# Starting each bank of sums with its own first product instead of a product of zeros, in a two-block transformer kernel on one Trainium2 core

## The chip, the cores and the metric

The kernel runs as one program on one core of a Trainium2 chip. The time is that of the device for one execution, in microseconds (us). Engines are named as in the profile: PE is TensorE's matmul side and PEld its weight load, DVE is VectorE, ACT is ScalarE, POOL is GpSimd, SP is SyncE. A stage is a run of weight units, as listed below.

## The reference

Two blocks of two layers each work on a sequence of 256 tokens with 1024 channels, batch 1, in float32. Cut to its products, the computation is:

```python
# first block
h = h + short_conv_mixer(rmsnorm(h), sc_w_in, sc_w_conv, sc_w_out)     # layer 0
h = h + squared_relu_mlp(rmsnorm(h), mlp_w_up[0], mlp_w_down[0])       # 1024 -> 4096 -> 1024
h = h + sigmoid(rmsnorm(h) @ ple_w_gate[0]) * (p[0] @ ple_w_proj[0])
h = h + dilated_attention_mixer(rmsnorm(h), positions, attn_w_qkv, attn_w_o)   # layer 1
h = h + squared_relu_mlp(...)
h = h + sigmoid(...) * (...)
x = rmsnorm(h, norm_final)
# second block
h = h + 0.5 * swiglu(rmsnorm(h), ffn1_w_in[0], ffn1_w_out[0])          # 1024 -> 2 x 2816 -> 1024
h = h + s5_mixer(rmsnorm(h), ...)                                      # state space, then a gated product
h = h + 0.5 * swiglu(rmsnorm(h), ffn2_w_in[0], ffn2_w_out[0])
kv = shared_kv(h, ...)
h = h + 0.5 * swiglu(rmsnorm(h), ffn1_w_in[1], ffn1_w_out[1])
h = h + nsa_mixer(rmsnorm(h), kv, w_qg, q_norm, w_o, rel_bias)         # sparse attention, 16 heads
h = h + 0.5 * swiglu(rmsnorm(h), ffn2_w_in[1], ffn2_w_out[1])
```

## The kernel before

**Units.** All large weight matrices are cut into 280 units of 128 x 2048 float32 numbers (1 MB each), used in a fixed order. The stages and their numbers of units are sc_in 12, sc_out 4, mlp0 32, ple0 5, qkv 36, wo 4, mlp1 32, ple1 5, ffn0 33, glu 4, ffn1 33, kv 6, ffn2 33, qg 4, nwo 4, ffn3 33. A unit comes through a ring of three slots: SP loads it (`raw`), ACT rounds it to float32r (`w_hi`, L1173), DVE subtracts to get the rest (`w_lo`, L1974), and PE uses both. ACT's step waits until PE is through with the unit three back (`unit_done`), PE waits for DVE's (`lo_ready`).

**Split products.** The activations are split the same way (`x_hi`, `x_lo`, ACT L1173 and DVE L1981). One product of a 128 x 128 block of weights and 256 tokens is made of three matmuls, in `exact` (L476 to L482): high by high (L480), high by low (L481), low by high (L482). A unit is 16 such triples, 48 matmuls of 256 columns.

**Banks of sums.** PSUM has eight banks of 128 x 512 float32, here called DB[0] to DB[3], U[0], U[1], MB and XB. A bank holds two blocks of 256 columns side by side (two blocks of output channels by 256 tokens). There are four ways in which units fill banks:
- `up_unit` without `arrive` (L529 to L535): first block over all eight chunks of the contraction, then the second block. Each block's first triple has start=True. No product of zeros.
- `up_unit` with `arrive` (L514 to L528), the first unit of a stage (13 calls: sc_out, mlp0, ple0, qkv, mlp1, ple1, ffn0, glu, ffn1, kv, ffn2, qg, ffn3): chunks outside, blocks inside, because the chunks of x arrive one pair after the other; before each pair PE waits for a semaphore (L518). Both blocks are open at once. The bank is begun by a product of zeros over its whole width, with start=True (L515), and every real product has start=False. It stands behind the wait for the unit's weights (`lo_ready`, L512) and ahead of the first wait for a chunk. `first_unit` (L496) does the same for the first of all.
- `down_unit` (L551): each unit adds two chunks of the contraction to all eight blocks of output, in DB[0] to DB[3], over 16 units (mlp) or 11 (ffn). Ahead of the first down unit of each mlp and ffn stage, `clear_sums` (L567) begins the four banks by four products of zeros. In `mlp` it stands behind the wait for `rs_ready` and ahead of the waits for `relu_ready` (L639 to L641), in `ffn` behind several waits (L688 to L695) and ahead of the down unit's own waits for weights and hidden values (L553, L554).
- The output projections of both attentions: `out_unit` (L877) adds to the four banks `WO` and begins each with a product of zeros (L888), in the first unit, behind a wait per bank. `out_part` (L1121) adds one chunk at a time to DB[2] and DB[3], begun at step 5 of the heads' loop (L1147); the third unit has DB[0], begun at L1159.

The product of zeros reads `zero`, a bfloat16 tile: 128 x 128 by 128 x 512. `clear_sums` has one more call, ahead of the S5 stage's sums (L917), and `keep_warm` (L572) makes such products at the start and around the S5 stage (26 + 20 + 6 + 24); `fin_sums` has a narrow one (L729).

**Order.** PE's order is written out by hand and has no planner. Between units stand the small products of norms (`norm_sum` L582, `norm_bcast` L588: sums over channels, then the spread of the result, with POOL and DVE between), the S5 tables' transposes (`table_turn`, L608, in mlp0 and mlp1), the attention's scores, transposes and values, and for the sparse attention a loop over 16 heads (L1139 to L1154) of `n_scores` (L1074 to L1079), `n_values` (L1106 to L1113), `n_turn` (L1093, L1094) and `out_part`. A stage ends with DVE adding the sums to h (L1987), ACT and DVE splitting the new x chunk by chunk, and the next stage's first unit taking each pair of chunks as it comes.

The split product and the clear in the code:

```python
nc.tensor.matmul(out, a_hi, b_hi, start=start, stop=False, skip_group_check=True)   # L480
nc.tensor.matmul(out, a_hi, b_lo, start=False, stop=False, skip_group_check=True)   # L481
return nc.tensor.matmul(out, a_lo, b_hi, start=False, stop=stop, skip_group_check=True)   # L482
...
for b in range(4):                                                                  # L569
    nc.tensor.matmul(DB[b], zero[:, 0:P], zero[:], start=True, stop=False, skip_group_check=True)
```

## Time and profile before

| | |
|---|---|
| median of 3 runs | 1874.66 us (1873.47 to 1879.29) |
| the profiled execution | 1871.93 us, of which the span is 1869.8 us |
| granted PE clock, mean over the span | 0.991 |
| PE busy | 1819.2 us (97%) in 15362 matmuls |
| DVE, ACT, POOL busy | 1202.9, 865.7, 627.8 us |
| DMA queues | 336.58 MB moved |

The span is cut from one profiled execution; the runs of the median were made without a profile. "Idle before" in a row is the time for which the engine did nothing before the instruction, with the instruction that ended it. Matmul rows overlap: a matmul of 256 columns has a duration of 0.28 us but the next one starts 0.11 to 0.12 us later, so costs are read from start to start. The matmul records of some products are missing from the trace, their weight loads (PEld) are there.

### The profile page before, as it was taken

The numbers are of one execution on the slowest core, as the hardware profiler recorded it, in microseconds if no ns is written. First come the engines' busy times: TensorE is split into PE (matmuls) and PEld (weight loads), VectorE is DVE, ScalarE is ACT, GpSimd is POOL, SyncE is SP. The second block draws the span as 40 slices with busy tenths as digits, with TensorE's granted clock in tenths as the row PEclk, the third lists the DMA queues.
The fourth block names the chain that finished last, engine by engine and source line by source line (L and its number), as shares of the span: only waits on it lengthen the run. The fifth ranks groups of instructions, "written<-read, shape, count | busy, mean of one in ns | idle before, by whom it ended". The sixth has DMA issues, their size and how long they took to land.

```text
span 1869.8 us, 35519 instructions
## 1 busy us (share of the span) xinstructions
PE 1819.2 (97%) x15362; PEld 1771.9 (95%) x15386; DVE 1202.9 (64%) x1380; ACT 865.7 (46%) x1096; POOL 627.8 (34%) x756
## 2 busy tenths in 40 slices
PE   8899999999999999999999889999999999999999
PEld 7899999999999999999999779999899999789999
DVE  7877667666664666686655855556655657756554
ACT  5254445544444544464344254344554446764442
POOL 6977781486752887010000620000000003530000
PEclk9999999999999999999999999999999999899999
DMA  7456665454444556557555416656346653024552
GB/s 262 171 203 217 220 230 190 156 180 170 159 167 155 182 208 219 200 207 305 181 183 211 148 47 217 216 211 216 137 136 209 216 199 124 23 69 181 184 194 97
DMA packets 53799, 336.58 MB, mean 180 GB/s; under 512 B 7899, under 2 KB 11020, under 8 KB 16908
## 3 DMA queue, kind: packets, MB, share of 16 engines
q1 hardware_dynamic: 46272, 300.00, 45.1%
q10 hardware_dynamic: 3276, 19.64, 2.9%
q0 software_dynamic: 4096, 14.68, 2.3%
q8 instruction: 121, 1.98, 0.4%
q14 instruction: 34, 0.28, 0.0%
HBM read 318.54 MB, written 15.75 MB: 179 GB/s over the span
## 4 chain that ended last, share of the span: by engine, by line
PE 83%; DVE 9%; ACT 4%; POOL 2%; issue 2%; DMA 1%; SPq 0%; ACTq 0%; DVEq 0%; POOLq 0%
PE psum L480 25%; PE psum L481 24%; PE psum L482 24%; DVE w_lo L1974 3%; ACT w_hi L1173 2%; DVE both L1981 1%; POOL swap L1891 1%; PE psum L1076 1%; PE psum L980 1%; ACT both L1173 1%; PE psum L942 1%; DVE yc L2312 1%; DVE h L1987 1%; PE psum L1093 1%; PE psum L1074 1%
## 5 line engine op out<-in xcount | busy, mean ns | idle before, releaser
L480 PE MATMUL psum<-both,w_hi 128*128 128x256 f32 x3584 | 1015.6, 283 | 21.7 <-DVE both L1981 12.8
L482 PE MATMUL psum<-both,w_lo 128*128 128x256 f32 x3584 | 1003.1, 280 | 0.0
L481 PE MATMUL psum<-both,w_hi 128*128 128x256 f32 x3584 | 1003.1, 280 | 0.0
L1974 DVE TENSOR_TENSOR w_lo<-raw,w_hi 128x2048 fp32r<-128x2048 f32 x277 | 655.7, 2368 | 287.7 <-ACT w_hi L1173 286.7
L1173 ACT ACTIVATE w_hi<-raw 128x2048 fp32r<-128x2048 f32 (+1 forms) x281 | 535.3, 1907 | 579.1 <-PE psum L482 561.1
L480 PEld LDWEIGHTS psum<-both,w_hi 128*128 128x128 f32 x3584 | 683.4, 191 | 26.6 <-DVE both L1981 15.7
L481 PEld LDWEIGHTS psum<-both,w_hi 128*128 128x128 f32 x3584 | 676.2, 189 | 0.9 <-issue 0.2
L482 PEld LDWEIGHTS psum<-both,w_lo 128*128 128x128 f32 x3584 | 675.4, 188 | 0.0
L1723 POOL TENSOR_TENSOR ssum<-sq 128x512 f32<-128x512 f32 x11 | 17.6, 1596 | 729.3 <-ACT sq L1197 729.3
L480 PE MATMUL psum<-hid_hi,w_hi 128*128 128x256 f32 x640 | 180.7, 282 | 0.0
L481 PE MATMUL psum<-hid_lo,w_hi 128*128 128x256 f32 x640 | 179.2, 280 | 0.0
L482 PE MATMUL psum<-hid_hi,w_lo 128*128 128x256 f32 x640 | 179.2, 280 | 0.0
L480 PEld LDWEIGHTS psum<-hid_hi,w_hi 128*128 128x128 f32 x640 | 122.3, 191 | 1.3 <-issue 0.8
L481 PEld LDWEIGHTS psum<-hid_lo,w_hi 128*128 128x128 f32 x640 | 120.2, 188 | 0.1
L482 PEld LDWEIGHTS psum<-hid_hi,w_lo 128*128 128x128 f32 x640 | 120.1, 188 | 0.0
L2111 DVE TENSOR_TENSOR tc<-psum,rs 128x512 f32<-128x512 f32 x44 | 30.4, 692 | 58.5 <-PE psum L482 58.5
L2105 DVE TENSOR_TENSOR ta<-psum,rs 128x512 f32<-128x512 f32 x44 | 30.4, 691 | 57.2 <-PE psum L482 56.3
L480 PE MATMUL psum<-w_hi,both 128*128 128x256 f32 x224 | 63.7, 284 | 1.4 <-DVE src L2525 1.4
L1895 POOL TENSOR_TENSOR qk<-qk,swap 32x512 f32<-32x512 f32 x24 | 63.6, 2651 | 1.9
L1891 POOL TENSOR_TENSOR swap<-swap,sin_rs 32x512 f32<-32x512 f32 x24 | 44.4, 1848 | 58.9 <-DVE swap L2384 58.9
L482 PE MATMUL psum<-w_hi,both 128*128 128x256 f32 x224 | 62.6, 279 | 0.0
L481 PE MATMUL psum<-w_lo,both 128*128 128x256 f32 x224 | 62.5, 279 | 0.0
(397 smaller groups left out, 2078.2 us busy)
## 6 DMA issues: line engine op xcount, KB each, us to landing
raw<-in_weights SPq DMA_DIRECT2D x279, 1024.0 KB, 4.8
table<-tables ACTq DMA_DIRECT2D x8, 1792.0 KB, 9.6
tables<-st POOLq DMA_DIRECT2D x16, 512.0 KB, 4.2
tables<-st POOLq DMA_DIRECT2D x8, 256.0 KB, 4.8
tables<-turns POOLq DMA_DIRECT2D x8, 256.0 KB, 4.4
w<-in_cmp_w ACTq DMA_DIRECT2D x4, 512.0 KB, 5.5
tbl<-in_cmp_w ACTq DMA_DIRECT2D x4, 512.0 KB, 5.6
tbl<-bias_v SPq DMA_DIRECT2D x128, 16.0 KB, 4.8
```

Source lines behind the costliest of these rows:

```text
L480: nc.tensor.matmul(out, a_hi, b_hi, start=start, stop=False, skip_group_check=True)
L481: nc.tensor.matmul(out, a_hi, b_lo, start=False, stop=False, skip_group_check=True)
L482: return nc.tensor.matmul(out, a_lo, b_hi, start=False, stop=stop, skip_group_check=True)
L942: last = nc.tensor.matmul(y_of(c, jj), x5[c % 2][:, ri, jj, 0:SK], q_[:, jj, ri], start=False, stop=ri == 1, skip_group_check=True)
L980: last = nc.tensor.matmul(DB[half][0:2 * NCMP, 0:P], blk[rows, l, :, :].rearrange("p c n -> p (c n)"), [w1, w1v][kind][rows, l, :], start= ...
L1074: nc.tensor.matmul(bank[:, 0:P], q[:, 0:P], ks[rows, br, a, 0:P], start=True, stop=True, skip_group_check=True)
L1173: copy = lambda out, in_, **kw: nc.scalar.activation(out, in_, ACT.Copy, **kw)
L1891: pool.tensor_tensor(swap[:], swap[:], sin_rs[0:32].unsqueeze(1).broadcast_to([32, 2, SEQ]), ALU.mult).then_inc(sem["sin_part"], 1)
L1895: pool.tensor_tensor(qk[0:32, side, gr], qk[0:32, side, gr], swap[:], ALU.add).then_inc(sem["qk_ready"], 1)
L1974: tt(w_lo[:, g % RING], raw[:, g % RING], w_hi[:, g % RING].bitcast(F32), ALU.subtract).then_inc(sem["lo_ready"], 1)
L2105: tt(ta[:], two(A_BANK), rs_b, ALU.mult).then_inc(sem["a_scaled"], 1)
L2111: tt(tc[:], two(B_BANK), rs_b, ALU.mult).then_inc(sem["b_gated"], 1)
```

## The change

A bank is begun by the first real product that goes into it: this product gets start=True, and the product of zeros in front is left out. Where two blocks of a bank are open together, only the first block's first triple starts; the second block's first triple keeps start=False. This is done in `first_unit`, in `up_unit` with `arrive`, in the down units of mlp and ffn (`down_unit` gets a flag `first`), in `out_unit`, in `out_part` and in the third unit of the last projection. The waits stay where they are. `clear_sums` stays for the S5 stage, as do `keep_warm` and `fin_sums`.

```diff
--- before.py
+++ after.py
@@ -496,7 +496,6 @@
             def first_unit(bank):
 
                 ws = slot(0)
-                nc.tensor.matmul(bank, zero[:, 0:P], zero[:], start=True, stop=False, skip_group_check=True)
                 for c in range(KC):
                     if c == KC // 2:
                         pe.wait_ge(sem["lo_ready"], 1)
@@ -504,7 +503,7 @@
                         pe.wait_ge(sem["xl_ready"], XBASE[R_IN] + c // 2 + 1)
                     for m in range(2):
                         last = exact(bank[:, m * SEQ:(m + 1) * SEQ], wide(ws, c, m),
-                                     (x_hi[0][:, c], x_lo[0][:, c]), False, c == KC - 1)
+                                     (x_hi[0][:, c], x_lo[0][:, c]), c == 0 and m == 0, c == KC - 1)
                 last.then_inc(sem["unit_done"], 1)
 
             def up_unit(g0, k, x, bank, arrive=None, mid=None, with_chunk=None):
@@ -512,13 +511,12 @@
                 pe.wait_ge(sem["lo_ready"], g0 + 1 + RING * k)
                 ws = slot(g0)
                 if arrive is not None:
-                    nc.tensor.matmul(bank, zero[:, 0:P], zero[:], start=True, stop=False, skip_group_check=True)
                     for c in range(KC):
                         if c % 2 == 0:
                             pe.wait_ge(arrive[0], arrive[1] + arrive[2] * (c // 2 + 1))
                         for m in range(2):
                             last = exact(bank[:, m * SEQ:(m + 1) * SEQ], wide(ws, c, m),
-                                         (x_hi[x][:, c], x_lo[x][:, c]), False, c == KC - 1)
+                                         (x_hi[x][:, c], x_lo[x][:, c]), c == 0 and m == 0, c == KC - 1)
                         if c == KC - 1:
                             last.then_inc(sem["unit_done"], 1)
                         if with_chunk is not None:
@@ -548,7 +546,7 @@
                         mid()
                 last.then_inc(sem["unit_done"], 1)
 
-            def down_unit(g0, k, hid_count, hid, tell=False, mid=None):
+            def down_unit(g0, k, hid_count, hid, first=False, tell=False, mid=None):
 
                 pe.wait_ge(sem["lo_ready"], g0 + 1 + RING * k)
                 pe.wait_ge(sem["hid_lo_ready"], hid_count)
@@ -557,7 +555,7 @@
                     for c in range(2):
                         cols = slice(c * D + m * P, c * D + (m + 1) * P)
                         last = exact(DB[m // 2][:, (m % 2) * SEQ:(m % 2 + 1) * SEQ], (wh[:, cols], wl[:, cols]),
-                                     (hid[0][:, c], hid[1][:, c]), False, c == 1)
+                                     (hid[0][:, c], hid[1][:, c]), first and m % 2 == 0 and c == 0, c == 1)
                     if tell and m % 2 and m < KC - 1:
                         last.then_inc(sem["acc_done"], 1)
                     if m == 3 and mid is not None:
@@ -637,14 +635,14 @@
                     up_unit(g + up_at(i), 0, x, mlp_bank(i))
                     if i == 2:
                         pe.wait_ge(sem["rs_ready"], n + 1)
-                        clear_sums()
                         pe.wait_ge(sem["relu_ready"], scaled + 2)
                     kernel = None
                     if i - 1 in TABLE_AT[l]:
                         c = 4 * l + TABLE_AT[l].index(i - 1)
                         table_turn(c)
                         kernel = lambda: table_kernel(c, scaled + 3)
-                    down_unit(g + down_at(i - 2), 0, hb + i - 1, hid_of(x, i - 2, MLP_PAIRS), mid=kernel)
+                    down_unit(g + down_at(i - 2), 0, hb + i - 1, hid_of(x, i - 2, MLP_PAIRS), i == 2,
+                              mid=kernel)
                 for i in range(MLP_PAIRS - 2, MLP_PAIRS):
                     down_unit(g + down_at(i), 0, hb + i + 1, hid_of(x, i, MLP_PAIRS), tell=i == MLP_PAIRS - 1)
 
@@ -693,8 +691,7 @@
                             pe.wait_ge(sem["fin_scale"], 1)
                         if f == 1:
                             pe.wait_ge(sem["bv_copied"], 1)
-                        clear_sums()
-                    down_unit(g + 4, k, hb + k + 1, hid_of(x, k, FFN_PAIRS))
+                    down_unit(g + 4, k, hb + k + 1, hid_of(x, k, FFN_PAIRS), k == 0)
                 down_unit(g + 3 * FFN_PAIRS - 1, 0, hb + FFN_PAIRS, hid_of(x, FFN_PAIRS - 1, FFN_PAIRS), tell=True)
 
             def ple(l, n):
@@ -885,13 +882,12 @@
                     if m == 0 and c == 0 and j % 2 == 0:
                         pe.wait_ge(*((sem["masked"], 4 * HEAD_PAIRS) if j == 4 else
                                      (sem["v_copied"], 3 * HEAD_PAIRS - 2 + [0, 1, None, 2][j // 2])))
-                        nc.tensor.matmul(WO[j // 2], zero[:, 0:P], zero[:], start=True, stop=False,
-                                         skip_group_check=True)
                     if done_after and c and j == 0:
                         pe.wait_ge(sem["o_lo"], HEADS)
                     cols = slice(c * D + j * P, c * D + (j + 1) * P)
                     last = exact(WO[j // 2][:, (j % 2) * SEQ:(j % 2 + 1) * SEQ], (wh[:, cols], wl[:, cols]),
-                                 (x_hi[1][:, 2 * m + c], x_lo[1][:, 2 * m + c]), False, done_after and c == 1)
+                                 (x_hi[1][:, 2 * m + c], x_lo[1][:, 2 * m + c]),
+                                 m == 0 and c == 0 and j % 2 == 0, done_after and c == 1)
                     if done_after and c and j % 2 and j < KC - 1:
                         last.then_inc(sem["acc_done"], 1)
                 last.then_inc(sem["unit_done"], 1)
@@ -1125,7 +1121,7 @@
                 for m in range(2):
                     for q in range(2):
                         last = exact(DB[2 + m][:, q * SEQ:(q + 1) * SEQ], wide(slot(g + m), ch, q),
-                                     (x_hi[0][:, ch], x_lo[0][:, ch]), False, ch == KC - 1)
+                                     (x_hi[0][:, ch], x_lo[0][:, ch]), ch == 0 and q == 0, ch == KC - 1)
                     if ch == KC - 1:
                         last.then_inc(sem["unit_done"], 1)
 
@@ -1143,9 +1139,6 @@
                     q_sums(3)
                 if step == 5:
                     pe.wait_ge(sem["q_var"], 5)
-                    for m in range(2):
-                        nc.tensor.matmul(DB[2 + m], zero[:, 0:P], zero[:], start=True, stop=False,
-                                         skip_group_check=True)
                 if step >= 4 and step % 2 == 0:
                     n_values((step - 4) // 2)
                 if step in OUT_AT:
@@ -1156,13 +1149,12 @@
             n_values(NQ - 1)
             pe.wait_ge(sem["lo_ready"], g + 3)
             pe.wait_ge(sem["n_log"], NH)
-            nc.tensor.matmul(DB[0], zero[:, 0:P], zero[:], start=True, stop=False, skip_group_check=True)
             for c in range(KC):
                 if c == 2:
                     out_part(KC - 1)
                 for q in range(2):
                     last = exact(DB[0][:, q * SEQ:(q + 1) * SEQ], wide(slot(g + 2), c, q),
-                                 (x_hi[0][:, c], x_lo[0][:, c]), False, c == KC - 1)
+                                 (x_hi[0][:, c], x_lo[0][:, c]), c == 0 and q == 0, c == KC - 1)
             last.then_inc(sem["unit_done"], 1)
             up_unit(g + 3, 0, 0, DB[1])
             ffn(3, R_NWO)
```

## Rows read from the trace of the kernel before

**Rows 1.** The page of the kernel before: busy time, and the chain by engine.

```profile
PE 1819.2 (97%) x15362; PEld 1771.9 (95%) x15386; DVE 1202.9 (64%) x1380; ACT 865.7 (46%) x1096; POOL 627.8 (34%) x756
...
PE 83%; DVE 9%; ACT 4%; POOL 2%; issue 2%; DMA 1%; SPq 0%; ACTq 0%; DVEq 0%; POOLq 0%
```

**Rows 2.** Instructions of one line: ns min/median/max, first to last start us.

```profile
L515 PEld LDWEIGHTS psum<-zero x13: 95/95/181, 86.9 to 1675.5; 128*128 128x128 bf16 x13
...
L570 PEld LDWEIGHTS psum<-zero x28: 95/98/101, 133.8 to 1701.6; 128*128 128x128 bf16 x28
```

**Rows 3.** PE's timeline at the last clear: start us, us, engine, line, operands.

```profile
1701.06 0.28 PE L482 MATMUL psum<-both,w_lo 128*128 128x256 f32 x1
1701.40 0.81 PE L570 MATMUL psum<-zero 128*128 128x512 bf16 x3
...
1702.16 0.28 PE L481 MATMUL psum<-hid_lo,w_hi 128*128 128x256 f32 x1
1702.28 0.28 PE L482 MATMUL psum<-hid_hi,w_lo 128*128 128x256 f32 x1
```

**Rows 4.** The same view in the attention projection's first unit.

```profile
577.58 0.28 PE L482 MATMUL psum<-both,w_lo 128*128 128x256 f32 x1
...
578.04 0.28 PE L481 MATMUL psum<-both,w_hi 128*128 128x256 f32 x1
```

**Rows 5.** The same view at ple0's first unit with arriving chunks.

```profile
310.45 0.28 PE L482 MATMUL psum<-p_hi,w_lo 128*128 128x256 f32 x1
...
310.91 0.28 PE L481 MATMUL psum<-both,w_hi 128*128 128x256 f32 x1
```

**Rows 6.** PE's timeline: waits inside or behind four first units.

```profile
94.42 0.39 PE L480 MATMUL psum<-both,w_hi 128*128 128x256 f32 x1 [3.03 <-DVE both L2325]
...
124.75 0.48 PE L588 MATMUL psum<-diag,ones 128*128 128x256 f32 x1 [0.72 <-DVE diag L2012]
...
607.44 0.39 PE L480 MATMUL psum<-both,w_hi 128*128 128x256 f32 x1 [1.59 <-DVE both L1981]
...
1679.45 0.39 PE L480 MATMUL psum<-both,w_hi 128*128 128x256 f32 x1 [0.80 <-DVE both L1981]
```

**Rows 7.** The chain that ended last, at L1147's zeros: start us, us, what.

```profile
1605.42 0.38 DVE lgc L2600 x2
...
1606.91 0.37 PE psum L1074
```

**Rows 8.** The chain at the last clear, and PE's timeline at ffn2's clear.

```profile
1701.40 0.81 PE psum L570 x3
...
1387.69 0.81 PE L570 MATMUL psum<-zero 128*128 128x512 bf16 x3 [0.69 <-ACT vcmp L1173]
```

**Rows 9.** Who waited for whom; PE's group of table transposes; ple1's first unit.

```profile
ACT w_hi L1173 <- PE psum L482: 561.1, 176, 5.0
...
PE psum L480 <- DVE w_lo L1974: 4.9, 4, 2.6
...
L608 PE MATMUL psum<-con,ab 128*128 128x128 f32 x64 | 8.3, 272 | 0.0
...
805.83 0.47 PE L480 MATMUL psum<-both,w_hi 128*128 128x256 f32 x1 [1.32 <-DVE w_lo L1974]
```

**Rows 10.** Windows (PEclk is third from the right), and PE's timeline and chain.

```profile
1586.40:1603.50 17.10, 17.10 (x74) 12.97 (x72) 13.71 (x39) 11.33 (x46) 12.57 (x17) 0.50 0.16 62
1603.50:1664.00 60.50, 57.34 (x457) 47.17 (x459) 38.01 (x121) 44.59 (x195) 24.60 (x45) 1.00 0.01 1
...
1586.26 0.72 PE L1079 MATMUL psum<-kcmp,q 64*128 64x15 f32 x4
...
1604.87 0.51 PE L1079 MATMUL psum<-kcmp,q 64*128 64x15 f32 x4
...
1616.68 0.51 PE L1079 MATMUL psum<-kcmp,q 64*128 64x15 f32 x4
...
1652.73 0.65 PE psum L1106 x4
```

## The prediction

> **What bounds the kernel now.** I read the page first. TensorE (PE) is busy for 1819.2 of 1869.8 us and holds 83% of the chain that ended last [rows 1]. So time taken out of PE counts wherever the chain lies on PE, and nowhere else. The question for each removed product is therefore a local one: does the chain run through it, or does PE, some microseconds later, wait for another engine anyway?
>
> For the count I took the weight loads of the zero products, because some of their matmul records are missing: 13 loads at L515 and 28 at L570 [rows 2], and in the same view of their own lines four at L888, one at L499, two at L1147 and one at L1159. That is 49 loads. Four of the 28 at L570 belong to the S5 stage (line 917), which the change leaves alone. So **45 products of zeros go**: 24 in the clears ahead of the first down units (4 in each of mlp0, mlp1, ffn0 to ffn3), 13 ahead of first units of stages, 4 in the attention projection, 2 + 1 in the last projection, 1 at the very start.
>
> **The price of one.** A clear in the dense stream: the last L482 before it starts at 1701.06, the second real product after it (L481) at 1702.16 [rows 3]. That is 1.10 us. Without zeros two steps of the stream lie there, each about 0.12 us (1702.16 to 1702.28 in the same rows), so four zeros cost 1.10 - 0.24 = 0.87 us, rounding aside, or 0.218 each. The group of three agrees: it lasts 0.81 us with 0.38 for its last product, so the starts are (0.81 - 0.38) / 2 = 0.215 us apart. A single zero in the attention projection: 577.58 to 578.04 is 0.46 us, less two steps of 0.12: 0.22 to 0.23 [rows 4]. A single zero ahead of a stage's first unit, whose own record is missing, shows the same hole: 310.45 to 310.91 is 0.46 us, so 0.23 [rows 5]. The 379 ns that a zero's own record lasts would be the upper bound per product, but these records overlap, and the next start is 0.215 behind. The lower bound is one slot of the real stream, 0.12 us. I take the measured holes.
>
> The Trainium skill ("TensorE: Matmul & The Clock Gate", section "Back-to-back issue gap") gives two figures for a product of 512 columns: about 216 ns by itself and about 131 ns in a sustained stream of loads and products. With the second, the count of 34 below would be worth an estimated 4.5 us. The trace agrees with the first [rows 3].
>
> **What lies on the path.** The removed products fall in two classes.
>
> Those that a wait behind them hides. When PE reaches the wait earlier, it waits longer. The waits behind them, with the idle time of PE just before the waiting product [rows 6]:
> - sc_out's first unit: 3.03 us until 94.42, for the convolution's last chunk;
> - mlp0's first unit: 0.72 us until 124.75, for the norm's diagonal, which is late because DVE makes two w_lo first;
> - mlp1's first unit: 1.59 us until 607.44, for the first chunk of the new sum;
> - the last ffn's: 0.80 us until 1679.45, for a later chunk.
> Five more look like the last two: the first unit of all, and those of qkv, ffn1, kv and qg. These are nine, each worth 0.22 us and each with at least 0.7 us of wait behind it, for DVE or ACT work that was begun earlier. The two at L1147 are hidden as well: the chain there is on DVE from 1605.42 and is back on PE at 1606.91 with L1074; the zeros and the transposes behind them run beside that [rows 7]. So 11 products are **costed at nothing**. If their cover were gone, they would add 11 x 0.22 = 2.4 us, the upper bound.
>
> Those on the chain, 34. The six clears: 6 x 0.87 = 5.2 us. The chain passes through all six (one piece of it stands in rows 8). At 1387.69 PE has waited for ACT's copy of vcmp, but that wait stands ahead of the clear, so the clear is paid too [rows 8]. The waits behind a clear are for the pair's hidden values and for relu; PE idles behind none of the six. The four in the attention projection: 4 x 0.23 = 0.9 us; PE goes straight on behind each [rows 4], and it idles at none of the last head's transposes that come between these units. Six first units: ple0 [rows 5], ple1, ffn0, glu, ffn2 and the bank of L1159, 6 x 0.23 = 1.4 us. In ple1 PE waited for w_lo, 1.32 us, but the zero came behind that wait and ahead of the first real product [rows 9], so it is paid.
>
> **Sum:** 5.2 + 0.9 + 1.4 = 7.5 us.
>
> **What is late next.** The weight ring must follow a faster PE. Its first step, ACT's w_hi, waits for PE in 176 cases (561 us in all), while PE waited for w_lo in only 4 [rows 9]. So the ring is paced by PE and moves with it. The POOL work that makes the S5 tables is not paced by the units, but PE idles 0.0 us ahead of the 64 transposes that need it [rows 9]; the unknown rest of that slack is part of rival 2. No DMA, semaphore or instruction of another engine is added or moved; PE's `pe.wait_ge` calls all stay in their order.
>
> **How that stands to the runs.** The profiled execution took 1871.93 us (span 1869.8); the median shown is 1874.66, with a spread from 1873.47 to 1879.29. I take the 7.5 us off the median: **1867.2 us**, 0.40% less. About 0.3%, 5.6 us, is what a measurement of this kernel can tell from no change, so the forecast lies only 1.9 us beyond it.
>
> **The rivals.**
> 1. *A zero is worth one slot of the stream, not 0.22.* What PE gets back may be less than the hole, if the first real product of a bank needs part of it anyhow: it lasts 0.47 us behind zeros against 0.28. At 0.12 us each, 34 are worth 4.1 us: 1870.6, no difference. Against it: a whole clear has only one such product and costs four times 0.218, so almost nothing of the hole belongs to the product behind. Chance 0.08. The skill's stream figure above would come out close to this.
> 2. *The saving is given back at the handovers.* Between stages the chain runs over DVE and ACT. If what arrives there (weights, POOL's norm, loads) keeps its own time, the savings of mlp0, ple0 and the projections are lost and about half is left, 3.7 us: 1871. For it: nine stage starts show such waits [rows 6]. Against it: they follow PE's last products of the stage before. Chance 0.13.
> 3. *The hidden ones count too.* 45 x 0.22 = 9.9 us: 1864.8. It needs waits that follow PE's own first unit. Chance 0.10.
> 4. *Slower: the clock.* From 1586.4 to 1603.5 PE runs at a granted clock of 0.50 (1.2 GHz), and at 1.00 (2.4 GHz) after that [rows 10]. The two zeros of L1147 stand at 1605.5, right behind the return, in the stage where PE's products are short. If without them and with more idle time PE stays low, the heads slow down: three steps take 1586.26 to 1604.87, 18.6 us, when low, and 1604.87 to 1616.68, 11.8 us, when full [rows 10], a factor of 1.58. From 1604.9 to the stage's last values at 1652.7 that is up to 47.8 x 0.58 = 27.7 us lost, less 7.5: 1895. It decides "slower" from 7.5 + 5.6 = 13.1 us of loss, about 23 us of the stage at the low level. Against it: PE was already back at full before the zeros came, and 0.43 us of zeros is little beside that. Chance 0.05.
> That the change doesn't do what it says is no rival of weight: each bank gets exactly one start, by the product that comes first in it.
>
> **How the numbers follow.** Forecast 0.62, the rivals 0.08, 0.13, 0.10, 0.05, and 0.02 for a median that is merely disturbed upwards. The forecast lies 1.9 us from the bound and medians move by more than a microsecond, so about 0.10 of its 0.62 would read as no difference. Faster: 0.52 + 0.10 + 0.02 from rival 2 = 0.64. Same: 0.10 + 0.08 + 0.11 = 0.29. Slower: 0.07. The range takes in the forecast with the scatter of the medians, rival 3 at its lower end and rivals 1 and 2 at its upper end: 1863 to 1873.
>
> **What would show it.** Right: 4 zero loads left at L570, none at the other lines but the warming ones; from the last L482 ahead of a first down unit to the second product in it 0.24 us instead of 1.10; PE busy less by 8 to 10 us; the waits of rows 6 longer by 0.2 us each; the stages mlp, ffn and wo shorter by about 0.9 us each and sc_in, sc_out, qkv, kv and qg not at all. Wrong: PE waits for w_lo in more than a handful of cases, a first real product of a bank that stays at 0.47 us behind a hole, or a low-clock stretch in the last projection that is longer than 17 us.

## The result, and the profile after

| | before | after |
|---|---|---|
| median of 6 runs | 1873.38 us (1872.33 to 1879.29) | 1844.83 us (1842.81 to 1851.37) |
| ratio, with its 95% interval | | 0.9849 (0.9828 to 0.987) |
| the profiled execution, its span | 1871.93, 1869.8 us | 1843.13, 1840.9 us |
| granted PE clock, mean over the span | 0.991 | 0.985 |

The change takes 28.5 us off the median, almost four times the 7.5 us of the forecast, and the time is below the range. In the changed kernel's own numbering w_hi is made at L1165 and w_lo at L1966; `exact` is still L480 to L482.

The page of the changed kernel: busy time and the chain by engine (as [rows 1]).

```profile
PE 1791.3 (97%) x15339; PEld 1741.8 (95%) x15341; DVE 1205.8 (65%) x1380; ACT 866.4 (47%) x1096; POOL 633.6 (34%) x756
...
PE 81%; DVE 8%; POOL 4%; ACT 4%; issue 2%; DMA 1%; SPq 0%; ACTq 0%; POOLq 0%; DVEq 0%
```

PEld has 15386 - 15341 = 45 weight loads fewer, exactly the removed products. But PE is busy for 27.9 us less, and 45 products at 0.22 us are 9.9 us. The rest cannot come from work that was taken away: all other products are the same ones in the same order.

**Where the place of the clear stands now.** PE's timeline of the changed kernel ahead of and in the last ffn's first down unit, as [rows 3].

```profile
1678.97 0.28 PE L482 MATMUL psum<-both,w_lo 128*128 128x256 f32 x1
...
1679.31 0.28 PE L482 MATMUL psum<-both,w_lo 128*128 128x256 f32 x1
1679.43 0.28 PE L480 MATMUL psum<-hid_hi,w_hi 128*128 128x256 f32 x1
1679.54 0.28 PE L481 MATMUL psum<-hid_lo,w_hi 128*128 128x256 f32 x1
1679.65 0.28 PE L482 MATMUL psum<-hid_hi,w_lo 128*128 128x256 f32 x1
```

From the last L482 ahead of the down unit to the unit's second product it is now 0.23 us (1679.31 to 1679.54) instead of 1.10: the clear's own 0.87 us is gone, as forecast. A triple (L482 to L482) takes 0.34 us on both sides. In the kernel before, the same view of the same stage, 11 us behind the clear:

```profile
1712.18 0.28 PE L482 MATMUL psum<-both,w_lo 128*128 128x256 f32 x1
...
1712.53 0.28 PE L482 MATMUL psum<-both,w_lo 128*128 128x256 f32 x1
...
1712.88 0.28 PE L482 MATMUL psum<-both,w_lo 128*128 128x256 f32 x1
...
1713.24 0.28 PE L482 MATMUL psum<-both,w_lo 128*128 128x256 f32 x1
```

A triple takes (1713.24 - 1712.18) / 3 = 0.353 us. **The stream has two paces.** A single pair of starts, rounded to 10 ns, hardly shows it; a count over a long window does. Windows of the kernel before, one in each of mlp1, ffn0, ffn1, ffn2 and ffn3 (window, its length, PE busy and matmuls, granted clock, DMA share, GB/s):

```profile
640.00:690.00 50.00, 50.00 (x438) 1.00 0.65 226
870.00:1010.00 140.00, 140.00 (x1191) 1.00 0.52 185
1160.00:1300.00 140.00, 140.00 (x1191) 1.00 0.62 217
1400.00:1540.00 140.00, 140.00 (x1238) 1.00 0.61 208
1720.00:1860.00 140.00, 140.00 (x1191) 1.00 0.46 164
```

The same five stages of the changed kernel (the last window takes in a wait at the end, 137.35 us of products):

```profile
640.00:690.00 50.00, 50.00 (x452) 1.00 0.61 218
860.00:1000.00 140.00, 140.00 (x1238) 1.00 0.55 195
1130.00:1270.00 140.00, 140.00 (x1238) 1.00 0.62 226
1370.00:1510.00 140.00, 140.00 (x1237) 1.00 0.62 210
1700.00:1840.00 140.00, 137.35 (x1212) 1.00 0.47 166
```

PE is busy all the time and at the full clock in both, yet 140 us hold 1191 products at the one pace and 1238 at the other: 117.5 against 113.1 ns each. From the starts within a unit the paces are 117.8 and 113.3 ns. They are sharp: in these stages every unit that nothing interrupts has the one or the other. A pace lasts until something interrupts the stream, mostly to the end of the stage. A unit of 48 products takes 5.65 us at the slower one and 5.44 at the faster, 0.21 us less. In ffn3 of the kernel before the pace changes at the clear. Windows of 10 us ahead of it and behind it (a count also takes in the products that are under way at the edges, so compare the two):

```profile
1690.40:1700.40 10.00, 10.00 (x91) 1.00 0.54 203
1702.40:1712.40 10.00, 10.00 (x87) 1.00 0.48 184
```

The weight loads show a small difference too. PE's loads of ffn1 (mean ns of one is the second number), before and then after:

```profile
L480 PEld LDWEIGHTS psum<-both,w_hi 128*128 128x128 f32 x332 | 63.7, 192 | 0.0
L482 PEld LDWEIGHTS psum<-both,w_lo 128*128 128x128 f32 x333 | 62.5, 188 | 0.0
```

```profile
L480 PEld LDWEIGHTS psum<-both,w_hi 128*128 128x128 f32 x349 | 65.5, 188 | 0.0
L482 PEld LDWEIGHTS psum<-both,w_lo 128*128 128x128 f32 x348 | 65.3, 188 | 0.0
```

Only the triple's first load differs, 192 against 188 ns; the matmul records last 281 against 276 ns.

**The ledger**, each stage from its first product to the next stage's first, before and after: mlp0 190.4 and 184.0, mlp1 191.3 and 185.0, ffn0 with the S5 stage 257.8 and 249.7, ffn1 195.2 and 188.0, ffn3 190.3 and 182.9: together 35.4 us less. mlp1's 6.3 are 25 units at 0.21 (5.3) and the clear (0.87); ffn3's 7.4 are 29 units (6.2) and the clear. ffn2, which ran at 113 ns before as well, gains 0.6, and wo 0.6. sc_in begins 0.9 us earlier (at 9.87 instead of 10.79), but sc_out still begins at 86.9, so nothing is gained there, and sc_out takes 0.6 us more. Against the gain stands qg with the last projection 7.8 us more (127.9 to 135.7), where the clock is low for longer. Windows of the changed kernel, as [rows 10]:

```profile
1558.00:1588.70 30.70, 30.25 (x126) 0.50 0.11 35
1588.70:1629.60 40.90, 38.01 (x299) 1.00 0.00 1
```

The stretch at a granted 0.50 (1.2 GHz) is 30.7 us long instead of 17.1.

### The profile page after: what moved, and what is told of

The parts are those of the page before. It is cut to its first block, busy times and chain, and to the rows that moved or that the text cites. A ratio compares the mean times of both kernels' runs of the same rounds, so it can differ in the third digit from the quotient of the medians.

```text
span 1840.9 us, 35461 instructions
## 1 busy us (share of the span) xinstructions
PE 1791.3 (97%) x15339; PEld 1741.8 (95%) x15341; DVE 1205.8 (65%) x1380; ACT 866.4 (47%) x1096; POOL 633.6 (34%) x756
## 4 chain that ended last, share of the span: by engine, by line
PE 81%; DVE 8%; POOL 4%; ACT 4%; issue 2%; DMA 1%; SPq 0%; ACTq 0%; POOLq 0%; DVEq 0%
PE psum L480 24%; PE psum L482 24%; PE psum L481 24%; DVE w_lo L1966 3%; ACT w_hi L1165 2%; DVE both L1973 1%; POOL swap L1883 1%; PE psum L1072 1%; PE psum L976 1%; ACT both L1165 1%; DVE yc L2304 1%; PE psum L1089 1%; DVE h L1979 1%; PE psum L1070 1%; POOL con L1926 1%
## 5 line engine op out<-in xcount | busy, mean ns | idle before, releaser
L480 PE MATMUL psum<-both,w_hi 128*128 128x256 f32 x3584 | 1004.4, 280 | 24.2 <-DVE both L1973 13.5
L481 PE MATMUL psum<-both,w_hi 128*128 128x256 f32 x3584 | 994.3, 277 | 0.0
L482 PE MATMUL psum<-both,w_lo 128*128 128x256 f32 x3584 | 994.3, 277 | 0.0
L1966 DVE TENSOR_TENSOR w_lo<-raw,w_hi 128x2048 fp32r<-128x2048 f32 x277 | 656.3, 2370 | 275.1 <-ACT w_hi L1165 274.6
L1165 ACT ACTIVATE w_hi<-raw 128x2048 fp32r<-128x2048 f32 (+1 forms) x281 | 536.0, 1910 | 547.0 <-PE psum L482 529.8
L480 PEld LDWEIGHTS psum<-both,w_hi 128*128 128x128 f32 x3584 | 675.9, 189 | 31.5 <-issue 12.3
L482 PEld LDWEIGHTS psum<-both,w_lo 128*128 128x128 f32 x3584 | 675.2, 188 | 0.0
L480 PE MATMUL psum<-hid_hi,w_hi 128*128 128x256 f32 x640 | 177.7, 278 | 0.5 <-ACT vcmp L1165 0.5
L482 PE MATMUL psum<-hid_hi,w_lo 128*128 128x256 f32 x640 | 176.8, 276 | 0.0
L480 PEld LDWEIGHTS psum<-hid_hi,w_hi 128*128 128x128 f32 x640 | 120.2, 188 | 1.4 <-issue 0.8
L482 PEld LDWEIGHTS psum<-hid_hi,w_lo 128*128 128x128 f32 x640 | 120.1, 188 | 0.0
L480 PE MATMUL psum<-w_hi,both 128*128 128x256 f32 x224 | 63.7, 284 | 1.4 <-DVE src L2517 1.4
L482 PE MATMUL psum<-w_hi,both 128*128 128x256 f32 x224 | 62.5, 279 | 0.0
```

Of the source, the lines that this page charges most:

```text
L1165: copy = lambda out, in_, **kw: nc.scalar.activation(out, in_, ACT.Copy, **kw)
L1966: tt(w_lo[:, g % RING], raw[:, g % RING], w_hi[:, g % RING].bitcast(F32), ALU.subtract).then_inc(sem["lo_ready"], 1)
```

## The experiments

The theory after the result: **the clear of four zeros, in a running stream, puts it on the 118 ns pace**, and that costs far more than the zeros themselves. Rivals: the start flag on a real product makes the bank faster, the other 21 removed zeros matter, the waits or the order of the three products set the pace. "Pace" below is the median from start to start within a unit, written 113 and 118 for short, and it is known only for the one profiled execution of each kernel. Except where runs are counted, a kernel ran once, beside the kernel before. Inserted products go to a bank that holds nothing at the time and are thrown away.

**1. Which removed zeros matter?** `e1_clears_back` is the changed kernel with the 24 zeros of the six clears put back; `e2_only_clears_gone` is the kernel before with these 24 alone gone.

```diff
 # e1, mlp; the same in ffn
+                        clear_sums()
-                    down_unit(..., hid_of(x, i - 2, MLP_PAIRS), i == 2, mid=kernel)
+                    down_unit(..., hid_of(x, i - 2, MLP_PAIRS), False, mid=kernel)
 # e2, against the kernel before
-                        clear_sums()
-                    down_unit(..., hid_of(x, i - 2, MLP_PAIRS), mid=kernel)
+                    down_unit(..., hid_of(x, i - 2, MLP_PAIRS), i == 2, mid=kernel)
```

> Base is the changed kernel; the 24 zero products ahead of the six first down units are put back, the other 21 stay away. Theory R (rhythm): the real products run in one of two rhythms, 113.3 or 117.8 ns from start to start; what stands in front of a stream decides which, and it holds to the next interruption; four zeros in a running stream set the slow one. Then the median spacing in mlp0, mlp1, ffn0, ffn1 and ffn3 behind the clear goes back to 117.8 and the time rises by about 5 us for the zeros and 20 to 24 us for the rhythm: 1868 to 1875 us. Rival S (the sum as predicted, the rest from elsewhere): only 5 us, near 1850 us, spacing 113.3.

> Base is the kernel before; only the 24 zero products ahead of the six first down units go, the 21 others stay. Theory R: nearly all of the 28.5 us, so 1845 to 1852 us, and 113.3 ns behind the clears. Rival S (each of the 45 products brings its share): 24/45 of 28.5 us, about 15 us, 1858 us. The forecast's own sum: 5 us, 1868 us.

e1: 1874.77 us (10 runs), 1.0008 (0.9994 to 1.0021) of the kernel before. e2: 1846.19 us (4 runs), 0.986 (0.9844 to 0.9877). So the gain is the clears'; the other 21 products bring at most 0.0006 x 1873 = 1.1 us, whether they lay on the chain or not. Windows of e1 in ffn0, ffn1, ffn2 and ffn3:

```profile
870.00:1010.00 140.00, 140.00 (x1192) 1.00 0.52 186
1160.00:1300.00 140.00, 140.00 (x1191) 1.00 0.61 215
1400.00:1540.00 140.00, 140.00 (x1238) 1.00 0.60 207
1720.00:1860.00 140.00, 140.00 (x1191) 1.00 0.44 159
```

The slower pace is back in the same stages, and again not in ffn2, where PE waits for vcmp ahead of the clear [rows 8]. In ffn1 the stream of e1 comes in at 113 and leaves the clear at 118 (10 us ahead of it and behind it):

```profile
1128.70:1138.70 10.00, 10.00 (x91) 1.00 0.46 165
1141.00:1151.00 10.00, 10.00 (x87) 1.00 0.46 170
```

**2. Is it the zeros' number, or that they are there?** `e3_one_zero` puts one zero at the six places in the changed kernel; `e4_clears_and_break` the four, and behind them one float32 product like the norm's spread. In both the real products keep their start flags.

```diff
 # e3
+                        keep_warm(1, DB[0])
 # e4
+                        clear_sums()
+                        nc.tensor.matmul(DB[0][:, 0:SEQ], ones[:], diag[:].rearrange("p t q -> p (t q)"),
+                                         start=True, stop=True, skip_group_check=True)
```

> The changed kernel with one zero product (512 columns, into DB[0]) at each of the six places where the clears were; the real products still start their banks, so nothing is computed otherwise. Theory R: the direct cost is 6 x 0.22 = 1.3 us; if it is the break by bfloat16 products in a running stream that sets the rhythm, one is enough: spacing 117.8 ns, about 1866 us. Rival (it is the phase that four of them leave): one may leave the fast one, 1846 us. Rival W (a bank begun by zeros takes sums more slowly): the banks are begun by real products here, so 113.3 ns and 1846 us.

> The changed kernel with all four zero products back at each of the six places and one more thrown-away float32 product of 256 columns (the one of the norm's spread, ones by diag) right behind them, into DB[0], which the real products then start afresh. Behind the norm's own such product the stream has run at 113.3 ns in every case of both traces. Theory R: the break resets the rhythm, so 113.3 ns in the five stages and only the direct cost, 6 x (0.87 + 0.3) = 7 us over the changed kernel: 1852 us, less work removed than in e1 and yet some 15 to 20 us faster. If the zeros themselves leave something behind that lasts: 117.8 ns and about 1875 us.

e3: 1850.22 us (2 runs, 1844.54 and 1855.9), 0.9873 (0.9837 to 0.991). e4: 1847.71 us (2 runs), 0.986 (0.984 to 0.988): it adds more work than e1 and is 27 us faster, though e1's real products have no start flag and e4's have, so the two differ in that as well. PE's timeline of e4 at ffn1's first down unit, where the stream came in at 118 ns:

```profile
1128.02 0.28 PE L482 MATMUL psum<-both,w_lo 128*128 128x256 f32 x1
1128.14 1.04 PE L568 MATMUL psum<-zero 128*128 128x512 bf16 x4
1129.01 0.59 PE L573 MATMUL psum<-diag,ones 128*128 128x256 f32 x2
1129.26 0.47 PE L480 MATMUL psum<-hid_hi,w_hi 128*128 128x256 f32 x1
```

And its windows in ffn0 and ffn3:

```profile
870.00:1010.00 140.00, 140.00 (x1235) 1.00 0.54 192
...
1700.00:1840.00 140.00, 140.00 (x1238) 1.00 0.47 166
```

1.24 us (1128.02 to 1129.26) go by between two real products here, and the stage behind them runs at 113 ns, as do mlp1, ffn0 and ffn3; only mlp0 ran at 118. That excludes the theory that a gap or the zeros' presence in itself slows the stream. The start flag is excluded by others: in e5 and e7 below the flags are there and the stream is at 118, and in ffn2 of the kernel before they are missing behind a clear and it is at 113 (1238 products in 140 us). PE's timeline of e3 at the same place:

```profile
1130.28 0.28 PE L482 MATMUL psum<-both,w_lo 128*128 128x256 f32 x1
1130.40 0.39 PE L573 MATMUL psum<-zero 128*128 128x512 bf16 x1
1130.44 0.47 PE L480 MATMUL psum<-hid_hi,w_hi 128*128 128x256 f32 x1
1130.74 0.28 PE L481 MATMUL psum<-hid_lo,w_hi 128*128 128x256 f32 x1
```

The zero costs 0.46 - 0.24 = 0.22 us here (1130.28 to 1130.74). In e3 it kept mlp1, ffn0 and ffn3 at 113 and turned ffn1 from 118 to 113, so one zero isn't enough for the slower pace, as the theory would have had it. But ffn2, which has a wait ahead of the place, came out at 118 (1191 products in 140 us), and so did mlp0, where the transposes of an S5 table stand right behind the place. Both also came out at 118 in kernels that had no zero there (ffn2 in e13 to e15, mlp0 in e6 to e8), so this need not be the zero's doing.

**3. The dose.** Each stage gets its own number of zeros; the second kernel exchanges the numbers between the stages.

```diff
+            for _ in range({"mlp1": 2, "ffn0": 3, "ffn1": 5, "ffn3": 6}.get(name, 0)):     # e5
+            for _ in range({"mlp1": 3, "ffn0": 2, "ffn1": 6, "ffn3": 5}.get(name, 0)):     # e6
+            for _ in range({"mlp1": 7, "ffn0": 8, "ffn1": 4, "ffn3": 12}.get(name, 0)):    # e15
+                nc.tensor.matmul(DB[0], zero[:, 0:P], zero[:], start=True, stop=True, skip_group_check=True)
```

> The changed kernel with zero products (512 columns) put in at the place of the clear in four stages whose stream is otherwise the same: 2 in mlp1, 3 in ffn0, 5 in ffn1, 6 in ffn3. Known so far: 0 and 1 leave the rhythm at 113.3 ns, 4 set 117.8 ns. Theory G (a gap of a certain length, or enough zeros in a row, sets the slow rhythm): one threshold, so 5 and 6 are slow for certain, 2 and 3 to one side of it. Theory P (what counts is the phase at which the stream goes on): fast and slow alternate with the number, for instance even slow and odd fast, with no threshold. Cost of a slow stage: 5.3 us (mlp1) or 6.1 us (ffn).

> The same with 3 in mlp1, 2 in ffn0, 6 in ffn1, 5 in ffn3. If the number decides, each number gives the rhythm that it gave in the other stage (2, 3, 5 and 6 each the same as in the run before). If the stage decides (what is in the units, the waits around), the stages keep theirs and the numbers don't matter.

> As e5, with 7 zero products in mlp1, 8 in ffn0, 4 in ffn1 and 12 in ffn3. Theory G' (a short run of 2 to 4 sets the slow rhythm, longer ones the fast one): 4 slow, 7, 8 and 12 fast. Theory P (phase): 7, 8 and 12 need not be alike, for instance slow again.

e5: 1851.92 us, e6: 1860.67, e15: 1869.39. With 2 and 3 zeros both stages ran at 118 (mlp1 with 2 until the transposes of an S5 table broke its stream), with 5 and 6 both at 113, also after the exchange: the number decides, not the stage, as far as two cases of each can show it. But it is no threshold: 7 gave 113, 8 and 12 gave 118, once each, and 4 left ffn1 at 118, where it was. Windows of e15 in mlp1 (7), ffn0 (8), ffn1 (4), ffn3 (12):

```profile
640.00:690.00 50.00, 50.00 (x452) 1.00 0.62 218
860.00:1000.00 140.00, 140.00 (x1191) 1.00 0.52 185
1150.00:1290.00 140.00, 140.00 (x1191) 1.00 0.61 215
...
1720.00:1860.00 140.00, 140.00 (x1191) 1.00 0.45 158
```

**4. Is it the kind of product, its width, or a wait?** `e7_real_products` and `e14_more_real` insert products like those of the stream (float32r, 256 columns); `e8_narrow_and_break` four zeros of 128 columns, or the float32 product alone; `e9_waits_only` waits that are met already.

```diff
+            for _ in range({"mlp1": 1, "ffn0": 2, "ffn1": 3, "ffn3": 4}.get(name, 0)):     # e7 (e14: 5, 6, 7, 8)
+                nc.tensor.matmul(DB[0][:, 0:SEQ], x_hi[x][:, 0, 0:P], x_hi[x][:, 0], start=True, stop=True, ...)
+            for _ in range({"mlp1": 4, "ffn0": 4}.get(name, 0)):                           # e8
+                nc.tensor.matmul(DB[0][:, 0:P], zero[:, 0:P], zero[:, 0:P], start=True, stop=True, ...)
+            if name in ("ffn1", "ffn3"):
+                nc.tensor.matmul(DB[0][:, 0:SEQ], ones[:], diag[:].rearrange("p t q -> p (t q)"), ...)
+            for _ in range({"mlp1": 1, "ffn0": 2, "ffn1": 4, "ffn3": 8}.get(name, 0)):     # e9
+                pe.wait_ge(sem["fill_done"], 4)
```

> The changed kernel with products of the stream's own kind (float32r, 128 x 128 by 256 columns, thrown away before the real product starts the bank) in place of zeros: 1 in mlp1, 2 in ffn0, 3 in ffn1, 4 in ffn3. If it takes the other type and length (bfloat16, 512 columns) to break the rhythm, all stay at 113.3 ns, and the time is the changed kernel's plus 10 x 0.113 = 1.1 us. If any additional product can (a count in the stream, its three loads per product being out of step), some of them go to 117.8 ns.

> As e7, with more thrown-away float32r products: 5 in mlp1, 6 in ffn0, 7 in ffn1, 8 in ffn3 (1, 2, 3 and 4 all led to 117.8 ns). If it is the number (as with the zeros, where 1, 5 and 6 lead to 113.3 ns and 2 to 4 to 117.8): some of these are fast, about 1843 to 1862 us. If it is the kind (any product of the stream's own kind put in front): all four slow, 5.3 to 6.1 us each, about 1868 us.

> The changed kernel with four bfloat16 zero products of only 128 columns in mlp1 and ffn0, and with one thrown-away float32 product (ones by diag) in ffn1 and ffn3. Theory G (length of the gap): 4 x 0.055 us is as short as one wide zero, so mlp1 and ffn0 stay fast. If the four loads and products of the other type count and not their length: slow, 5.3 and 6.1 us. The float32 product leaves ffn1 and ffn3 fast by either theory, since it set the fast rhythm from the slow one in e4; if it merely turns one rhythm into the other, both go slow.

> The changed kernel with waits of PE on a semaphore that was reached long before (fill_done), at the place of the clear: 1 in mlp1, 2 in ffn0, 4 in ffn1, 8 in ffn3. No product and no weight load is added. If the rhythm depends on what PE's array and loads do (a load or product out of step), all four stages stay at 113.3 ns, and the time is the changed kernel's. If it depends on how the instructions come to PE (their number, a bubble in their issue), some go to 117.8 ns and cost 5.3 to 6.1 us each.

e7: 1867.74 us, e14: 1876.88, e8: 1854.6, e9: 1844.98. Behind each number of real products from 1 to 8 the stream was at 118, so even one more product of the stream's own kind does it. (The 3 in ffn1 met a stream that was at 118 already, and the 1 in mlp1 held only until the transposes of a table.) Four narrow zeros left mlp1 and ffn0 at 113. The float32 product alone turned ffn1 from 118 to 113, but ffn3 from 113 to 118: what an interruption leaves seems to depend on the pace it meets, by one case each way. Windows of e8 in ffn1 and ffn3:

```profile
1150.00:1290.00 140.00, 139.48 (x1231) 1.00 0.62 222
...
1700.00:1840.00 140.00, 140.00 (x1191) 1.00 0.47 166
```

Waits that are met changed the pace nowhere in e9: mlp1, ffn0 and ffn3 stayed at 113, and ffn1 was at 118 ahead of the place and stayed there.

**5. Does the order of the three products hold the pace?** In the kernel before, the second and third change places.

```diff
-                nc.tensor.matmul(out, a_hi, b_lo, start=False, stop=False, skip_group_check=True)
-                return nc.tensor.matmul(out, a_lo, b_hi, start=False, stop=stop, skip_group_check=True)
+                nc.tensor.matmul(out, a_lo, b_hi, start=False, stop=False, skip_group_check=True)
+                return nc.tensor.matmul(out, a_hi, b_lo, start=False, stop=stop, skip_group_check=True)
```

> The kernel before, with its clears, and the second and third product of each triple exchanged (high by high, low by high, high by low), so that the two with the same weights don't follow each other. In the slow rhythm it is the load for L480, behind low by high, that takes 192 ns where the others take 188. If the slow rhythm hangs on that order, the stages behind the clears run at 113.3 ns: about 1850 us. If the order has no part in it: 117.8 ns and 1874 us.

1872.61 us, with the paces of the kernel before, ffn3 at 118 for 29 of 33 units. The order has no part in it.

**6. The longer low clock, and the scatter.** `e10_warm_heads` adds two zeros ahead of the transposes of heads 0 to 7; `e11_changed_again` and `e18_changed_third` are the changed kernel once more.

```diff
+                if hd <= 7:                                                                # e10
+                    for br in range(2):
+                        nc.tensor.matmul(U[br], zero[:, 0:P], zero[:], start=True, stop=True, skip_group_check=True)
```

> The changed kernel with two zero products (512 columns) ahead of the transposes of heads 0 to 7 in the sparse attention, into the banks that the transposes then write. In the changed kernel the granted clock is 0.50 for 30.7 us there, in the kernel before for 17.1 us; qg and nwo together take 135.7 us against 127.9. If more work on PE keeps the clock up: the stretch at 0.50 is under 10 us and the two stages take 122 to 128 us, in spite of up to 3.5 us for the zeros. If it doesn't: 3.5 us more than the changed kernel's other runs.

> The changed kernel again, unaltered. Theory R: mlp1, ffn0, ffn1 and ffn3 are at 113.3 ns again, since nothing between their last norm product and the first down unit varies; mlp0, whose stream is broken by four table turns, may come out in either rhythm (5.5 us), as it did with the same code in the other runs, and the stretch at the low clock in the sparse attention varies by some us. So 1843 to 1851 us.

> The changed kernel, unaltered, beside the two: median 1843 to 1848 us, with single runs 6 us or more higher where ffn1, ffn2 or mlp0 come out in the slow rhythm.

e10: 1841.37 us (2 runs), 0.9834 (0.9796 to 0.9872), low stretch 17.1 us, qg and last projection 131.7; expected were under 10 us and 122 to 128. e11: 1848.3 us (2 runs, 1842.42 and 1854.18), low stretch 30.7, qg and last projection 135.8. e18: 1843.82 us (5 runs), 0.9859 (0.9833 to 0.9884), low stretch 20.5, qg and last projection 129.7. So the stretch differs between executions of one kernel; how much of it the change brings can't be told, and e10's gain isn't shown. In e18 all 33 units of ffn1 ran at 118 (194.5 us), in e11 only the first two (188.0): same code, other pace. It was decided in the second unit, where the norm's spread stands; what came in at the place of the clear went on. mlp0, ffn2 and glu, which have waits or small products just ahead or behind, also came out at either pace. A whole ffn at the other pace is 6 us, so this can account for most of the scatter of the changed kernel's runs, 1842 to 1854; the runs without a profile don't show their paces.

**7. Can the pace be set on purpose?** By e3 one wide zero in a running stream may lead to 113 from either pace. `e13_kept_fast` adds to e10 one zero in mlp0 and one in ffn1; `e16_held` adds to the changed kernel one in mlp0 and one in each ffn, all in the running stream of a later unit; `e17_held_and_warm` has e10's zeros as well.

```diff
 # e16, in mlp and in ffn
+                    if i == 2 and l == 0:
+                        keep_warm(1, mlp_bank(i))
...
+                    if k == 1:
+                        keep_warm(1, A_BANK)
```

> The kernel of e10 (two zero products ahead of the transposes of heads 0 to 7), and one zero product (512 columns) each where the stream may stand in the slow rhythm in some executions: ahead of mlp0's third unit and ahead of ffn1's first down unit. One zero left the stream fast in five cases, from the slow rhythm too (ffn1 in e3). If one zero leads to the fast rhythm from either: ffn1 at 113.3 ns in its later units always and mlp0 as in the changed kernel, median 1838 to 1843 us and under 1846 us in nearly all runs. If it is no better than chance: some runs 6 us or 12 us higher, as the changed kernel has them.

> The changed kernel with five zero products (512 columns) put in where the stream runs without idle time: ahead of mlp0's third unit, and ahead of the sixth unit of each ffn stage (k = 1). One zero in a running stream led to 113.3 ns from 113.3 (three cases) and from 117.8 (two). If it always does: all of ffn0 to ffn3 at 113.3 ns from their sixth unit on, in every execution; median 1842 to 1845 us, no run over about 1849 us, against up to 1854 us for the changed kernel. If not: as wide a scatter as the changed kernel's, and 1 us more.

> e16 and e10 together: the zeros ahead of heads 0 to 7 as well. If both work: 1838 to 1842 us, the fastest of all. If the zeros in the heads only happened to meet a short stretch at the low clock in e10: as e16 or up to 3.5 us more.

e13: 1848.21 us (4 runs), 0.9865 (0.9849 to 0.9882): its zero turned ffn1 from 118 to 113, but in its profiled execution ffn2 came out at 118 (197.4 us), where it had no zero, and its median is above the 1838 to 1843 us expected. e16: **1841.14 us** (5 runs, 1838.56 to 1843.35), 0.983 (0.981 to 0.985). e17: **1840.99 us** (4 runs, 1839.74 to 1841.89), 0.983 (0.9811 to 0.9848). Windows of e16 in mlp1 and the four ffn:

```profile
640.00:690.00 50.00, 50.00 (x452) 1.00 0.62 217
860.00:1000.00 140.00, 140.00 (x1237) 1.00 0.54 196
1140.00:1280.00 140.00, 139.34 (x1230) 1.00 0.61 222
1380.00:1520.00 140.00, 139.14 (x1228) 1.00 0.60 206
1690.00:1830.00 140.00, 140.00 (x1238) 1.00 0.47 170
```

All run at 113. But the four ffn streams of this execution were at 113 ahead of their zeros as well, so only mlp0, which its zero turned from 118 to 113, shows a turn here. In e17 the same happened in mlp0, and ffn1 was at 118 ahead of its zero and at 113 from it on. Five zeros more, and the kernel is faster than the kernel before by 31 us and its runs lie within 5 us. Against the changed kernel (e18, on the same chip, 1843.82) the medians are 2.7 us apart and the intervals overlap. Of the 13 runs of the changed kernel 5 took 1849 us or more, of the 9 of e16 and e17 none took more than 1843.4. That points to the zeros but doesn't show it: the counts are small, and the 13 runs come from three sets of runs. e17's extra zeros bring nothing that can be seen.

## Why the prediction was wrong

Point by point, in the prediction's order.

- **The count and the price of the zeros: right.** 45 loads are gone, and the clear's hole is 0.87 us shorter. A single zero in a running stream costs 0.22 us too, in e3's timeline. The isolated figure of the Trainium skill ("TensorE: Matmul & The Clock Gate", section "Back-to-back issue gap"), about 216 ns, fits that.
- **"Without zeros two steps of the stream lie there, each about 0.12 us": this is the step that failed.** It is right for the hole and was taken as if the stream's pace were a constant of the kernel. Every removed clear was costed at its own duration, and the 29 units behind it at nothing. What these units got back was 5.3 to 6.2 us a stage: the term "six clears, 5.2 us" came out as some 35 us in the profiled executions, and as 27.4 us in the medians (e2). PE was busy for 27.9 us less, not for 8 to 10. The trace of before had it: in mlp1, ffn0 and ffn3 the one or two units right ahead of the clear run at 113.3 ns and those behind it at 117.8, but single gaps rounded to 10 ns (0.11 and 0.12) were read as one number. That the change is faster at all was forecast rightly, but most of the gain is by a mechanism that the prediction doesn't have.
- **The four in the attention projection and the six first units, 2.3 us: too much.** wo is 0.6 us shorter, ple0 0.3, ple1 and glu about 0.1. In the median the 21 products together stay below 1.1 us (e1).
- **The hidden ones at nothing: right in kind.** The waits behind them grew in two cases (sc_out 3.03 to 3.29, mlp1 1.59 to 1.69 us), stayed at 0.72 in mlp0 and shrank in the last ffn (0.80 to 0.53).
- **"The ring must follow": right.** PE waited for w_lo in 6 cases, 5.6 us, against 4 and 4.9 [rows 9], though PE now eats a unit in 5.44 instead of 5.65 us.
- **Rivals 1 to 3** priced the same holes differently and miss the mechanism alike. Rival 2's handovers gave back little: the 0.9 us at the start and 0.6 us in sc_out.
- **Rival 4, the clock: its place was right and its price smaller.** The low stretch was 30.7 us long and that stage 7.8 us longer, against the 13.1 us named for a slower kernel. A stretch over 17 us was named as a sign of being wrong, and it came. Other executions of the same code had 20.5 us and gave most of it back.
- No rival said that a removed product could change the speed of those that stay. The range had no room for it.

The scatter of ffn1 and mlp0 blurs two terms. The kernel before ran all of ffn1 at 118 in its profiled execution, ahead of the clear too, and so did e18 without a clear. In mlp0 the stream of before was at 118 ahead of the clear, ran at 113 for the 24 products behind it, and was at 118 again from a table's small products in the middle of that unit on; without a clear mlp0 came out at 118 in e6, e7 and e8. So about 12 of the 35 us are not the removed clears' for certain. In mlp1, ffn0 and ffn3 the pace changed from 113 to 118 at the clear in each of the three traces with clears alone (before, e1, e12), and in e1 it did so in ffn1. That the clears together are worth some 27 us in the median rests on e1 and e2, not on this ledger.

**What stays open:** why one interruption leaves the stream at one pace and another at the other, and why it comes out either way behind waits and, in ffn1, behind a short stretch at a granted 0.50 (1122.2 to 1125.6 us in the kernel before). The counts (1, 5, 6, 7 zeros to 113; 2, 3, 4, 8, 12 to 118; none leaves the pace that is there) look like a matter of how weight loads and products come to lie against each other. That was not shown; the one difference between the loads is the first one's 192 against 188 ns. The Trainium skill ("TensorE: Matmul & The Clock Gate", section "Back-to-back issue gap") says that in a stream load and product together set the spacing, and no run here tells whether that is the reason.

## What to carry to other kernels

Before costing an edit in a dense stream at its own duration, count the stream's products over 100 us or more on both sides of the place: 4% of pace over a stage outweighs the edit. A stream that is busy throughout and at full clock can still have a slower pace, so compare like stages with each other (ffn2's 1238 against 1191 in 140 us was there to be seen). Where an interruption can't be left out, try what a single thrown-away product behind it does, and time it in several runs, since the same code can come out either way.

## What the runs showed that was not expected

- Two sharp paces of one stream of 256-column products, 113.3 and 117.8 ns from start to start at a granted clock of 1.00, held for as long as a whole stage of 190 us.
- Adding work can make the kernel faster: e4, with four zeros and a float32 product in each of six places, takes 1847.71 us, and e1, with the four zeros alone (and no start flags behind them), 1874.77.
- Inserted products set the pace by number and kind, not by the time they take: four zeros and a float32 product, a hole of 1.24 us, left 113, and one product of the stream's own kind 118. Waits that are met didn't touch it (e9).
- The low-clock stretch in the stage of short products was 3.4 us (e17) to 30.7 us (e11) long from one execution or kernel to the next.
